# A hybrid decoder step on one core: the samples' token tile and the gates computed with two products instead of three

## The reference

```python
h = rms_norm(x, norm1_g)
proj = h @ w_in          # q, k, v of 8 heads; q/k raw, v, output gate of 4 mLSTM heads; 8 gate columns
x = x + concat(dilated_attention(q, k, v), mlstm(conv(qk_raw), v, gates + b_gate)) @ w_out
h2 = rms_norm(x, norm2_g)
x = x + square(relu(h2 @ w_up)) @ w_down      # 1024 -> 4096 -> 1024
y = rms_norm(x, norm_f_g)
```

## Time and profile before

| | |
|---|---|
| median of 3 runs | 3032.68 us (3024.05 to 3034.35) |
| profiled execution | 3033.52 us, its span 3031.8 us |
| mean granted clock of PE | 0.982 |
| busy share of the span | PE 96%, PEld 82%, DVE 47%, POOL 33%, ACT 31% |

### The profile page before, as it was taken

How to read it: one execution, slowest core, us unless ns; L and a number is a source line. 1 busy time by engine, 2 the same in 40 slices (tenths; PEclk the granted TensorE clock), 3 DMA queues, 4 the chain that set the end, 5 groups by cost and what they waited for, 6 DMA issues and landing times.

```text
span 3031.8 us, 47808 instructions
## 1 busy us (share of the span) xinstructions
PE 2897.2 (96%) x18451; PEld 2494.0 (82%) x18451; DVE 1415.6 (47%) x3340; ACT 926.7 (31%) x1741; POOL 998.5 (33%) x558
## 2 busy tenths in 40 slices
PE   7999999999999978889999999999999999999998
PEld 5878788887777756678799999989999998988886
DVE  5522555223888845586343333344333333544443
ACT  4301322111767742422132221233222213422222
POOL 1212011210445530210063443444434344544443
PEclk8999999999999988989999999999999999999999
DMA  4322223335364447955352322235223223533332
GB/s 135 111 101 96 95 93 121 101 105 154 123 202 149 159 141 316 380 170 182 116 224 105 123 94 106 94 118 222 92 106 115 101 106 114 201 138 131 118 121 82
DMA packets 124795, 421.43 MB, mean 139 GB/s; under 512 B 18655, under 2 KB 44387, under 8 KB 104918
## 3 DMA queue, kind: packets, MB, share of 16 engines
q1 hardware_dynamic: 103836, 366.53, 34.2%
q10 hardware_dynamic: 19658, 48.68, 4.1%
q0 software_dynamic: 1152, 4.19, 0.5%
HBM read 350.83 MB, written 135.63 MB: 160 GB/s over the span
## 4 chain that ended last, share of the span: by engine, by line
PE 47%; DVE 1%; ACT 1%; DMA 1%; POOL 1%; issue 0%; ACTq 0%; DVEq 0%
PE mlp_bank L209 16%; PE mlp_bank L210 16%; PE mlp_bank L211 16%; POOL mlp_wu_lo L2580 0%; DMA mlp_acc<-x 0%; DMA mlp_xb<-x 0%; DVE mlp_acc L2797 0%; DVE mlp_acc L2813 0%; PE mlp_bank L2903 0%; DVE mlp_xn L2784 0%; DMA out_y_prompt<-mlp_acc 0%; POOL mlp_xb L2618 0%; ACT mlp_acc L2709 0%; ACT mlp_wu_hi L2634 0%; ACT mlp_xn L2718 0%
## 5 line engine op out<-in xcount | busy, mean ns | idle before, releaser
L2797 DVE TENSOR_TENSOR mlp_acc<-mlp_acc,mlp_bank 128x512 f32<-128x512 f32 (+1 forms) x544 | 349.3, 683 | 382.9 <-PE mlp_bank L211 382.7
L209 PE MATMUL mlp_bank<-mlp_hT_hi,mlp_wu_hi 128*128 128x384 f32 (+1 forms) x1536 | 496.7, 323 | 2.4 <-PEq L3039 2.4
L211 PE MATMUL mlp_bank<-mlp_hT_hi,mlp_wu_lo 128*128 128x384 f32 (+1 forms) x1536 | 495.4, 322 | 0.0
L210 PE MATMUL mlp_bank<-mlp_hT_lo,mlp_wu_hi 128*128 128x384 f32 (+1 forms) x1536 | 495.1, 322 | 0.0
L2784 DVE TENSOR_TENSOR mlp_xn<-mlp_xn 128x384 f32<-128x384 f32 (+1 forms) x192 | 204.2, 1070 | 511.0 <-ACT mlp_xn L2652 491.6
L209 PE MATMUL mlp_bank<-mlp_wd_hi,mlp_u_hi 128*128 128x512 f32 (+1 forms) x1088 | 425.6, 391 | 6.8 <-DVE mlp_acc L2797 6.8
L210 PE MATMUL mlp_bank<-mlp_wd_lo,mlp_u_hi 128*128 128x512 f32 (+1 forms) x1088 | 424.7, 390 | 0.0
L211 PE MATMUL mlp_bank<-mlp_wd_hi,mlp_u_lo 128*128 128x512 f32 (+1 forms) x1088 | 424.3, 390 | 0.0
L2584 POOL TENSOR_TENSOR mlp_wd_lo<-mlp_wd_raw,mlp_wd_hi 128x2048 fp32r<-128x2048 f32 x48 | 221.9, 4623 | 404.3 <-ACT mlp_wd_hi L2640 404.3
L2592 POOL TENSOR_TENSOR mlp_u_lo<-mlp_xn,mlp_u_hi 128x384 fp32r<-128x384 f32 (+1 forms) x192 | 182.5, 963 | 362.1 <-ACT mlp_u_hi L2661 362.0
L209 PEld LDWEIGHTS mlp_bank<-mlp_hT_hi,mlp_wu_hi 128*128 128x128 f32 x1536 | 288.8, 188 | 5.4 <-issue 2.8
(11 more groups left out here) (348 smaller groups left out, 4599.8 us busy)
## 6 DMA issues: line engine op xcount, KB each, us to landing
mlp_wu_raw<-in_w_up SPq DMA_DIRECT2D x48, 1024.0 KB, 4.8
mlp_wd_raw<-in_w_down SPq DMA_DIRECT2D x48, 1024.0 KB, 4.9
out_win_k_sample<-in_cache_k SPq DMA_DIRECT2D x48, 680.0 KB, 6.4
out_win_v_sample<-in_cache_v SPq DMA_DIRECT2D x48, 680.0 KB, 7.3
p_w_raw<-in_w_tok SPq DMA_DIRECT2D x10, 2048.0 KB
sm_vin<-in_cache_v SPq DMA_DIRECT2D x8, 2048.0 KB, 12.6
proj<-p_stage ACTq DMA_DIRECT2D x53, 256.0 KB, 2.0
parts<-mx_part SPq DMA_DIRECT2D x48, 264.0 KB, 4.3
```

The source lines that it names most:

```text
L209: nc.tensor.matmul(out, ah, bh, start=(k == 0), stop=False)
L210: nc.tensor.matmul(out, ah, bl, start=False, stop=False)
L211: ins = nc.tensor.matmul(out, al, bh, start=False, stop=(k == n - 1))
L2797: ins = v.tensor_tensor(acc[0:rows, t, 512 * e:512 * e + 512], acc[0:rows, t, 512 * e:512 * e + 512], bank[4 + 2 * (t % 2) + e][0:rows, :] ...
```

## The change

For the tiles and pieces named above, the low part is put beside the high part in one stationary operand, and two matmuls run where three did: stacked x moving high, stacked x moving low. The product low x low is computed too. The output has the high part's rows in one place of the partitions and the low part's in another, and DVE adds the two.

- Gates: one tile `wg` of 40 columns, the high part repeated in columns 0 to 31, the low part in 32 to 39. Output on partitions 0 to 39; DVE adds partitions 32 to 39 after the bias.
- Tile 16 in project: the low part is written by `dve_lo_beside` to `hT_lo` and to columns 64 to 127 of `hT_hi`'s last tile, four DVE instructions of 128x256 for two of 128x512. In `tile_out` of that tile DVE copies partitions 64 to 127 of the bank to partitions 0 to 63 of `xn` and adds them to the bank, each step waiting for the one before, ahead of the rotary work.
- Tile 16 in project_out: the low part goes to columns 64 to 127 of `mT_hi`; `add_last` adds both halves of the bank, four DVE instructions for two.
- Tile 16 in mlp: `split_u` writes the last 64 columns of `u_lo`'s second half to `u_hi` behind the high part (two POOL instructions for one, in two of four pieces of each block). The bank's 128 partitions are added to `acc` as for the other tiles for blocks 0 to 14, `fold` adds partitions 64 to 127 of `acc` to 0 to 63 after block 14, and `add_last` of block 15 adds both halves of the bank, four DVE instructions for two.

```diff
+def stacked_products(nc, out, triples, last_inc=None, before=None, part=None):
+    n = len(triples)
+    for k in part or range(n):
+        a, bh, bl = triples[k]
...
+        nc.tensor.matmul(out, a, bh, start=(k == 0), stop=False)
+        ins = nc.tensor.matmul(out, a, bl, start=False, stop=(k == n - 1))
...
+    def dve_lo_beside(self, dve, T, s, col, w):
+        dve.wait_ge(self.hi_ready, T + 1)
+        for half in range(2):
+            k = slice(4 * half, 4 * half + 4)
+            src = self.tr[2 * s + half][:].rearrange("p (k c) -> p k c", k=4)[:, :, 0:w]
+            for dst in (self.lo[:, k, col:col + w], self.hi[:, k, col + w:col + 2 * w]):
+                last = self.nc.vector.tensor_tensor(dst, src, self.hi[:, k, col:col + w].bitcast(F32), ALU.subtract)
+        last.then_inc(self.lo_ready, 1)
...
+                if GT0[g] + t == TILES - 1:
+                    chain.link(v.tensor_copy(xn[0:NS, 1, 512:1024], bank[2 + s][NS:2 * NS, :]))
+                    chain.link(v.tensor_tensor(bank[2 + s][0:NS, :], bank[2 + s][0:NS, :], xn[0:NS, 1, 512:1024], ALU.add))
...
-                    v.tensor_scalar(stage[0:8, q, 0:w], bank[GB[q]][0:8, 0:w], bg[:, 0:1], None, ALU.add).then_inc(gate_ready, 1)
+                    chain.link(v.tensor_scalar(stage[0:8, q, 0:w], bank[GB[q]][0:8, 0:w], bg[:, 0:1], None, ALU.add))
+                    v.tensor_tensor(stage[0:8, q, 0:w], stage[0:8, q, 0:w], bank[GB[q]][LO_AT:LO_AT + 8, 0:w],
+                                    ALU.add).then_inc(gate_ready, 1)
...
+                    if GT0[g] + t == TILES - 1:
+                        stacked_products(nc, bank[2 + (n * j + t + g) % 2][:],
+                                         [(hT_hi[:, k, t * P:(t + 1) * P], w_hi[j][:, k], w_lo[j][:, k])
+                                          for k in range(KC)], tok_mm, split)
+                        continue
...
+            def add_last():          # project_out
+                x, part = xt[NP % 3], slice(0, NS)
...
+                for e in range(2):
+                    dve.wait_ge(prod_mm, 2 * NP + e + 1)
+                    cols, ps = slice(512 * e, 512 * e + 512), bank[4 + 2 * (NP % 2) + e]
+                    chain.link(v.tensor_tensor(x[part, cols], x[part, cols], ps[0:NS, :], ALU.add))
+                    v.tensor_tensor(x[part, cols], x[part, cols], ps[NS:2 * NS, :], ALU.add).then_inc(added, 1)
...
+                    end = w * q + w  # split_u
+                    cols = slice(w * q, end - NS if g == G - 1 and q else end)
+                    ins = g_.tensor_tensor(u_lo[s][:, m, cols], u2[:, m, cols], u_hi[s][:, m, cols].bitcast(F32), ALU.subtract)
+                    if g == G - 1 and q:
+                        ins = g_.tensor_tensor(u_hi[s][:, m, end:end + NS], u2[:, m, end - NS:end],
+                                               u_hi[s][:, m, end - NS:end].bitcast(F32), ALU.subtract)
+                    ins.then_inc(u_lo_ready, 1)
...
+            def fold():
+                t = GN[G - 1] - 1
+                dve.wait_ge(summed, GN[G - 1] * FB - GN[G - 1] + DB[G - 1])
+                chain.link(v.tensor_copy(gain2[0:NS], acc[NS:2 * NS, t]))
+                chain.link(v.tensor_tensor(acc[0:NS, t], acc[0:NS, t], gain2[0:NS], ALU.add))
+            def add_last():          # mlp
+                t = GN[G - 1] - 1
+                dve.wait_ge(down_mm, GN[G - 1] * FB + DB[G - 1])
+                for part in (slice(0, NS), slice(NS, 2 * NS)):
+                    for e in range(2):
+                        cols = slice(512 * e, 512 * e + 512)
+                        ins = v.tensor_tensor(acc[0:NS, t, cols], acc[0:NS, t, cols],
+                                              bank[4 + 2 * (t % 2) + e][part, :], ALU.add)
+                    if part.start == 0:
+                        chain.link(ins)
+                ins.then_inc(summed, 1)
...
                     add(g, 14)
-                    for t in range(GN[g]):
+                    fold()
+                    for t in range(GN[g] - 1):
                         add(g, 15, (t,))
                         if t:
                             last_root(t - 1)
+                    add_last()
+                    last_root(GN[g] - 2)
                     last_root(GN[g] - 1)
...
+                        if GT0[g] + t == TILES - 1:
+                            stacked_products(nc, bank[4 + 2 * (t % 2) + e][:],
+                                             [(u_hi[s][:, m, t * P:(t + 1) * P], wd_hi[s][:, m, 512 * e:512 * e + 512],
+                                               wd_lo[s][:, m, 512 * e:512 * e + 512]) for m in range(2)], down_mm if e else None)
+                            continue
```

More of the change, by code:

```diff
@@ L38 @@
 TOP = REC_AT + REC
+LO_AT = 32
 LN_EXP = "natural_log_exp_and_others"
@@ L214, in split_products @@
     return ins
+def stacked_products(nc, out, triples, last_inc=None, before=None, part=None):
+    n = len(triples)
+    for k in part or range(n):
+        a, bh, bl = triples[k]
+        if before:
+            before(k)
+        nc.tensor.matmul(out, a, bh, start=(k == 0), stop=False)
+        ins = nc.tensor.matmul(out, a, bl, start=False, stop=(k == n - 1))
+    if last_inc is not None and k == n - 1:
+        ins.then_inc(last_inc, 1)
+    return ins
 def project(K):
@@ L374, in _ @@
             pool.wait_ge(wg_hi_ready, 1)
-            nc.gpsimd.tensor_tensor(wg_lo[:], wg_raw[:], wg_hi[:].bitcast(F32), ALU.subtract).then_inc(wg_lo_ready, 1)
+            nc.gpsimd.tensor_tensor(wg[:, :, LO_AT:LO_AT + 8], wg_raw[:], wg[:, :, 0:8].bitcast(F32),
+                                    ALU.subtract).then_inc(wg_lo_ready, 1)
             def lo(E, dst, hi, src):
@@ L418, in constants @@
                 act.wait_ge(const_in, 16 * 7)
-                nc.scalar.activation(wg_hi[:], wg_raw[:], ACT.Copy).then_inc(wg_hi_ready, 1)
+                nc.scalar.activation(wg[:, :, 0:LO_AT].rearrange("p k (r c) -> p k r c", c=8),
+                                     wg_raw[:].rearrange("p k (r c) -> p k r c", r=1).broadcast_to([P, KC, LO_AT // 8, 8]),
+                                     ACT.Copy).then_inc(wg_hi_ready, 1)
                 act.wait_ge(pe_state, 1)
@@ L682, in _ @@
                 if g == 0:
-                    norm.dve_lo(dve, 2 * n, 0, n * P)
+                    norm.dve_lo_beside(dve, 2 * n, 0, n * P, NS)
         @block.tensor
@@ L690, in gates @@
                 at, w = GC[g][q], GW[g][q]
-                split_products(nc, bank[GB[q]][0:8, 0:w],
-                               [(wg_hi[:, k], wg_lo[:, k], hT_hi[:, k, at:at + w],
-                                 hT_lo[:, k, at:at + w]) for k in range(KC)], gate_mm, part=part)
+                stacked_products(nc, bank[GB[q]][0:LO_AT + 8, 0:w],
+                                 [(wg[:, k], hT_hi[:, k, at:at + w], hT_lo[:, k, at:at + w]) for k in range(KC)],
+                                 gate_mm, part=part)
             def first(g, q, part=None):
@@ L2353, in lo @@
                 for e in range(2):
-                    ins = v.tensor_tensor(O.mT_lo[:, p, 4 * e:4 * e + 4, 0:w],
+                    dst = O.mT_lo[:, p, 4 * e:4 * e + 4, 0:P] if t < NP else O.mT_hi[:, p, 4 * e:4 * e + 4, NS:2 * NS]
+                    ins = v.tensor_tensor(dst,
                                           bank[2 * p + e][:].rearrange("p (k c) -> p k c", k=4)[:, :, 0:w],
@@ L2389, in _ @@
             for t in range(NP + 2):
-                if 0 <= t - 1:
+                if 0 <= t - 1 < NP:
                     add(t - 1)
+                elif t - 1 == NP:
+                    add_last()
                 if t + 2 < NP:
@@ L2443, in products @@
                     pe.wait_ge(added, 2 * t + e - 3)
+                if t == NP:
+                    stacked_products(nc, bank[4 + 2 * p + e][:],
+                                     [(O.mT_hi[:, p, k], O.w_hi[:, k, 512 * e:512 * e + 512],
+                                       O.w_lo[:, k, 512 * e:512 * e + 512]) for k in range(KC)], prod_mm)
+                    return
                 split_products(nc, bank[4 + 2 * p + e][0:w, :],
@@ L2790, in add @@
                 for t in tiles or range(n):
-                    rows = P if GT0[g] + t < TILES - 1 else NS
                     done = n * f + (DB[g] + t)
@@ L2796, in add @@
                     for e in range(2):
-                        ins = v.tensor_tensor(acc[0:rows, t, 512 * e:512 * e + 512], acc[0:rows, t, 512 * e:512 * e + 512],
-                                              bank[4 + 2 * (t % 2) + e][0:rows, :], ALU.add)
+                        ins = v.tensor_tensor(acc[:, t, 512 * e:512 * e + 512], acc[:, t, 512 * e:512 * e + 512],
+                                              bank[4 + 2 * (t % 2) + e][:], ALU.add)
                     ins.then_inc(summed, 1)
+            def fold():
[14 more added lines that the diff above has]
+                ins.then_inc(summed, 1)
             def final(g):
@@ L2910, in down @@
                 for t in range(n):
```

(1 more changed line is left out.)

11 lines of the change are left out of this document (4 added, 7 removed).

## The result

The changed kernel takes 2996.73 us (median of 4 runs, 2989.50 to 3000.71) where the kernel before took 3028.36 in 4 runs beside it (3022.37 to 3034.35): ratio 0.9893, 95% interval 0.9862 to 0.9924, 31.6 us between the medians. The profiled execution after took 2989.5 us, its span is 2987.7. The forecast was 3002 in a range of 2994 to 3012. It was counted from a median of 3032.7 in three runs; the kernel before has a median 4.3 us lower here, which is most of the 5 us between 3002 and 2996.73, and the gain is 0.8 us larger than forecast.

The account below looks back on a forecast made before the run. PE was taken as the bound, busy 2897.2 of 3031.8 us. Gates 6.9, tokens 7.7, project_out 2.9 and down 13.3 sum to 30.8 us, so 3032.7 - 30.8 = 3002 us, range 2994 to 3012.

Parts of the forecast that it names:

- The price of a matmul: On PE, a 512-column matmul costs 0.227 to 0.231 us whether the stationary operand has 8, 64 or 128 columns.
- stacked matmuls are dearer: Rival for all stacked matmuls: 0.26 us each instead of 0.23, 9.6 us in all, about 3011; chance 0.06.
- a matmul taken away is worth less than the distance: Rival on PE: the third product ran partly beside the others, gross gain 19.4 us instead of 33.5, 3016; chance 0.01.
- Gates: Gates in project: 8 of 24 matmuls fewer in each of 5 pieces, 2.9 us in g=0 and 4.0 in g=1, 6.9 together.
- Tokens: Tile 16's tokens in project: 9.1 us of matmuls less 1.4 for copy and add at the stage's end, 7.7 us.
- project_out: Tile 16 in project_out: 16 matmuls fewer, 3.6 us, less 0.7 for one more add before the barrier, 2.9 us.
- down: Tile 16 in mlp's last group: 0.93 us a block, 13.9 over blocks 0 to 14, less 0.6 in the tail, 13.3.
- the mlp part doesn't arrive: Rival in mlp: a wait for weights or POOL's split takes its place in each block, 3015 us; chance 0.07.
- The clock: PE's low clock behind the two barriers: its stretch may change by 1.7 us each; 0 taken, -3.4 to +3.4 kept.

Follow-up runs that it names:

- e4: Changed kernel with a third matmul (stacked x moving low again) per stacked pair, so as many matmuls as the kernel before: 3030.34 us, ratio 0.9999.
- e7: The changed kernel with no edit, timed again with more rounds against the kernel before: 2992.95 us, ratio 0.9892.
- e3: Only the project part of the change, mlp and project_out as in the kernel before: 3019.53 us, ratio 0.9961.
- e5: Changed kernel with tile 16 first instead of last in the second group's last token block: 2996.22 us in one run.
- e6: Changed kernel, tile 16 first in last token block; mlp's last group: alternating bank pairs, fold after block 13, tile 16 second in block 15: 2994.68 us, ratio 0.9891.
- e10: The e6 kernel profiled once more with no further edit, for the spread of stage lengths: span 2987.4 us.
- e2: Only the mlp part of the change, project and project_out as in the kernel before: 3013.26 us, ratio 0.9943.

## Why the prediction was right, step by step

**The price of a matmul** was right, but one reading under it was off: the 5.44 us of the earlier trace rows are the 24 matmuls of tile 16, which has 64 stationary columns, and not a row for 128, nor one of the loop of down. DVE takes up the tile before those two at 722.01, so the 24 matmuls between that and 727.45 have 128 stationary columns, and they take 5.44 us too:

```profile
722.01 0.30 DVE L630 TENSOR_TENSOR p_bank<-p_bank,p_rot 128x128 f32<-128x128 f32 x1 [3.96 <-PE p_bank L211]
```

So the statement on the width was right, with a row that hadn't been shown. The 16 matmuls of gates (0,1) stand at 0.234 us, and tile 16 of down takes 1.81 for the 1.83 forecast. e4 shows the reverse: put the third matmuls back, at 128 columns, and the whole gain is gone, to 0.9999. The rivals "stacked matmuls are dearer" and "a matmul taken away is worth less than the distance" fall with that. So does the figure of 131 ns of the Trainium skill (TensorE: Matmul & The Clock Gate, Back-to-back issue gap) for these operands: the traces show 0.227 to 0.234 us in every form at 512 columns and a granted clock of 1.00.

**Gates**, forecast 6.9. In g=0, from the turn of tile 4 to where PE, behind `first` and one block of `chunk`, waits for POOL's low part of the next q/k weights, 39.59 us became 36.62 (means of three): 3.0 for 2.9. In g=1, from the turn of tile 15 to the same place (the second block of `chunk`), 38.8 became 35.4: 3.4 for 4.0. Of the missing 0.6, 0.5 went into a wait that I had not looked at, PE's for POOL's low part of those q/k weights at the end of that stretch, 1.5, 1.0 and 1.0 us before, 1.7, 1.7 and 1.6 after.

```profile
403.32 0.49 PE L220 MATMUL p_bank<-p_hT_hi,p_w_hi 128*128 128x512 f32 x1 [1.69 <-POOL p_w_lo L404]
```

The chain on POOL doesn't become shorter with PE's, so part of the gain ahead of it is handed over to the wait; this term of the sum was sized 0.5 too large, and the wait should have been in the list of what is late next.

**Tokens**, forecast 7.7. From there, so from the second block of `chunk` in g=1, to the mixers 326.9 us became 318.8, so 8.1; only the token tiles in it changed. Blocks 0 to 3 hide the copy and the add as said, and the barrier grew by the 1.4 that were said. Gates and tokens give 14.5 of 14.6; project as a whole has 13.9 since two of the three traces of after take 21.9 us for a stretch at the start of g=1 that takes 20.5 in all other traces of the two: behind a wait of PE of 2.32 us they have a granted clock of 0.57 over 4 us, the others 1.00. In e7:

```profile
320.00:324.00 4.00, 4.00 (x14) 3.16 (x13) 1.71 (x7) 2.53 (x6) 0.00 (x0) 0.57 0.62 199
```

That is the clock that is low in one execution and not in the next, as behind the barrier of project_out; after, e3, e5, e6 and e10 have the same change and 20.5.

**project_out**, forecast 2.9: 3.0, with a spread of about 1 us in each kernel. **down**, forecast 13.9 less 0.6: 14.3 less 0.45. The first small wait of the last group (0.31 us) went too, which is most of the 0.4 more. `wd_lo` of the next block stayed hidden, `fold` is over 1.25 us before DVE is needed, and the wait ahead of down(15) stayed at 1.47. So "the mlp part doesn't arrive" is out; e2 has it alone at 17.4 us between medians, more than its own 13.9 and well within its interval of 11.5 to 22.7.

**What was not in the sum** is 3.5 us in group 1, which all three traces of after have and whose cause is open. With them and group 0's 0.5 the stages gain 34.8 us without the mixers; timed are 31.6 and 33.2 us, with intervals that hold the 30.8 as well as the 34.8. So the forecast's steps are shown by the stages, and that the timed total comes within 1 to 3 us of their sum is no further proof. The clock, for which I kept 3.4 either way, was low behind project's barrier in every trace, and came out at both values behind that of project_out in both kernels.

## What to carry to other kernels

When PE is the bound and a small tile leaves half of the stationary columns empty, put the low part of that operand there, beside its high part: the matmul costs the same 0.23 us and one of three products goes. Pay attention to the ends of the stages, since the halves still have to be added, and an add that is free in a loop costs its whole time ahead of a barrier. Before crediting an edit with a gain in a stage that it doesn't touch, profile both kernels three times: here single spans differed by 44.1 us where the medians differed by 31.6.
